# Two transformer-like blocks on one core: the end of the first block's experts, rebuilt, and the order of the second block's first slabs

## What is computed, cut to what matters here

```python
# peer_ffn, per token block of 128: for 8 heads the 16 best of 16384 experts
ue = jnp.take(u, eid, axis=0)
act = jax.nn.gelu(jnp.einsum('thkd,td->thk', ue, xt), approximate=False)
ve = jnp.take(v, eid, axis=0)
ff = jnp.einsum('thk,thkd->td', gate * act, ve)
h = layernorm(ALPHA * h + ff, ln2_g, ln2_b)      # end of block 1, ALPHA = 2 ** 0.25
x = h                                            # block 2
h = rmsnorm(x, norm1_gain_2); proj = h @ w_in_2
q_a, f_a, i_a, g_a, q_b, k_b, v_b, f_b = jnp.split(proj, ...)
```

## Time and profile before

| | |
|---|---|
| median of three runs | 3098.26 us |
| the profiled execution's own time | 3097.76 us |
| its span in the trace, mean granted clock | 3096.0 us, 0.985 |
| PE, PEld busy | 2666.7 us (86%), 1914.2 us (62%) |
| DVE, ACT, POOL busy | 1770.5 us (57%), 881.6 us (28%), 532.5 us (17%) |
| the chain that ended last | PE 60%, DMA 30%, DVE 5%, issue 3% |
| bytes moved | 859.94 MB, of them 536.90 by POOL's gathers |

### The profile page before, as it was taken

The page is one execution under the profiler, slowest core; times in us unless marked ns, Lnnn a source line. Parts: engine busy times, 40 slices in busy tenths (PEclk is TensorE's granted clock), DMA queues, the critical chain, the costliest instruction groups (busy, mean ns, idle before and its releaser), DMA issues.

```text
span 3096.0 us, 33400 instructions
## 1 busy us (share of the span) xinstructions
PE 2666.7 (86%) x12561; PEld 1914.2 (62%) x12561; DVE 1770.5 (57%) x2212; ACT 881.6 (28%) x943; POOL 532.5 (17%) x532
## 2 busy tenths in 40 slices
PE   6999998677777777777777777999999999999998
PEld 6999888622222222222222237998877888888886
DVE  5456556855555555555555456544656656555445
ACT  3433433300011111111111004433444444444443
POOL 0000000344433343333334430000000000000000
PEclk9999999899999999999999998999999999999999
DMA  6554563899999999999999995544454555555553
GB/s 228 169 172 160 180 228 136 341 422 421 421 422 422 422 422 422 422 422 422 422 422 422 422 356 179 175 156 151 143 190 155 189 190 189 189 189 190 190 193 146
DMA packets 220040, 859.94 MB, mean 278 GB/s; under 512 B 17616, under 2 KB 20016, under 8 KB 147120
## 3 DMA queue, kind: packets, MB, share of 16 engines
q0 software_dynamic: 73728, 536.90, 41.9%
q1 hardware_dynamic: 146224, 321.79, 31.1%
HBM read 856.54 MB, written 2.10 MB: 277 GB/s over the span
## 4 chain that ended last, share of the span: by engine, by line
PE 60%; DMA 30%; DVE 5%; issue 3%; ACT 1%; POOL 0%; POOLq 0%; DVEq 0%; ACTq 0%
DMA vb<-in_peer_v,vidx 29%; PE PS L462 11%; PE PS L2002 7%; PE PS L1860 7%; PE PS L464 5%; PE PS L491 5%; PE PS L495 5%; PE PS L493 5%; PE PS L503 4%; PE PS L507 4%; PE PS L505 4%; DVE wl L396 1%; ACT wh L391 1%; DMA ub<-in_peer_v,vidx 1%; PE PS L1876 1%
## 5 line engine op out<-in xcount | busy, mean ns | idle before, releaser
L1860 PE MATMUL PS<-vb,diag 128*128 128x512 f32 x1920 | 890.0, 607 | 331.4 <-DMA vb<-in_peer_v,vidx 317.3
L396 DVE TENSOR_TENSOR wl<-raw,wh 128x2048 fp32r<-128x2048 f32 x292 | 669.3, 2292 | 732.0 <-ACT wh L391 730.4
L1860 PEld LDWEIGHTS PS<-vb,diag 128*128 128x128 f32 x1920 | 346.3, 190 | 874.4 <-issue 750.6
L1358 DVE CUSTOM_DVE_ANT_0 ub<-ub,RES 128x2048 f32<-128x2048 f32 x256 | 586.5, 2292 | 479.0 <-DMA ub<-in_peer_u,uidx 475.1
L391 ACT CAST wh<-raw 128x2048 fp32r<-128x2048 f32 x292 | 556.7, 1907 | 912.8 <-PE PS L495 292.7
L462 PE MATMUL PS<-XHL,wh 128*128 128x512 f32 x1408 | 488.2, 394 | 0.0
L491 PE MATMUL PS<-XHL,wh 128*128 128x256 f32 x1408 | 402.2, 286 | 7.8 <-DVE XHL L537 4.8
L495 PE MATMUL PS<-XHL,wl 128*128 128x256 f32 x1408 | 399.6, 284 | 0.0
L493 PE MATMUL PS<-XHL,wh 128*128 128x256 f32 x1408 | 399.6, 284 | 0.0
L464 PE MATMUL PS<-XHL,wl 128*128 128x256 f32 x1408 | 390.0, 277 | 0.0
L689 POOL DMA_INDIRECT ub<-in_peer_u,uidx x256 | 261.9, 1023 | 648.2 <-DVE uidx L1346 528.7
(11 more groups left out here) (304 smaller groups left out, 2166.6 us busy)
## 6 DMA issues: line engine op xcount, KB each, us to landing
raw<-in_w_in SPq DMA_DIRECT2D x112, 1024.0 KB, 5.1
raw<-in_w_ffn_gate SPq DMA_DIRECT2D x44, 1024.0 KB, 5.2
raw<-in_w_ffn_up SPq DMA_DIRECT2D x44, 1024.0 KB, 5.1
raw<-in_w_ffn_down SPq DMA_DIRECT2D x44, 1024.0 KB, 4.8
raw<-in_w_out SPq DMA_DIRECT2D x32, 1024.0 KB, 5.1
raw<-in_peer_wq SPq DMA_DIRECT2D x16, 1024.0 KB, 5.1
ub<-in_peer_u,uidx POOLq DMA_INDIRECT x256, 16.5
vb<-in_peer_v,vidx POOLq DMA_INDIRECT x240, 15.3
```

Of the source, the lines that this page charges most:

```text
L396: dve.tensor_tensor(wl[u % 2][:], raw[u][:], wh[u % 2][:].bitcast(F32), ALU.subtract).then_inc(lo_full[u % 2], 1)
L1358: dve.tensor_tensor_reduce(ub[k % RING][:], ub[k % RING][:], RES[:, tb, :], 1.0, 0.0, ALU.mult, ALU.add, dots[:, tb, k:k + 1]).then_inc(S. ...
L1860: m = pe.matmul(PS[:, 4 * tb + b, :], diag[:, k, :], vb[k % RING][:, b * W:(b + 1) * W], start=start and k == 0, stop=False, skip_group_ch ...
```

## The change

- The four units of block 2's first slab are loaded before the experts; ACT and DVE split units 0 and 1 inside the expert stage (ACT after step 1, DVE after step 1 and after step 13). GAIN3 moves to another place (PH + 40, the scores of tb 1) and is loaded after the last selection (`uidx_ready` 16).
- Before the first v row PE writes ALPHA times RES into all eight banks, with a scaled identity (`adiag`). DVE's scaling of RES goes.
- DVE takes rows 13 and 14 of the last step, PE row 15. DVE's first row is a plain product.
- Token block 0: statistics and centring read PSUM. Token block 1: DVE adds bank by bank as PE's last row finishes each, statistics between. Both norms go in quarters of 512 columns, ACT squares each scaled quarter and sums it, NRM is made in quarters and turned quarter by quarter.
- PE multiplies units 0 and 1 for token block 0 before it turns token block 1, then for token block 1.
- Block 2's slabs come in the order v v f f q q; the steps of the recurrent mixer are one unit apart, from slab 6 unit 3 on instead of slab 5 unit 3.

`mm_tokens` is `mm_unit`'s token form for one token block, split off. DVE's and PE's plans of the second block shift as ACT's do. `wf_raw` and slab 1 now follow `last_full[1]` at once.

```diff
-DVE_ROWS = (5, 7, 9, 11, 14, 15)
+DVE_ROWS = (5, 7, 9, 11, 13, 14)
...
-GATES2, HEADS2, ATTN = 7, 11, 43
+GATES2, HEADS2, ATTN = 7, 27, 43
...
-    GAIN3 = at("GAIN3", 56, [D])
+    GAIN3 = at("GAIN3", PH + 40, [D])
+    adiag = at("adiag", PH + 48, [P])
...
+        w_in2 = w_view(inp["w_in_2"])
+        for u in range(UNITS):
+            load_unit(sp, S_IN2, u, w_in2[:, u * UC:(u + 1) * UC, 4 * W:5 * W])
         sp.wait_ge(S.scores_cp, 8)
         sp.dma_start(GAIN[:], row(inp["ln2_g"][0], D)).then_inc(S.norm_in, 16)
         sp.dma_start(BIAS[:], row(inp["ln2_b"][0], D)).then_inc(S.norm_in, 16)
-        sp.wait_ge(w_free[1], 2 * S_IN2)
+        sp.wait_ge(S.uidx_ready, 2 * H)
         sp.dma_start(GAIN3[:], row(inp["norm1_gain_2"][0], D)).then_inc(S.norm_in, 16)
         sp.wait_ge(last_full[1], 16 * (TOPK // RING))
-        w_in2 = w_view(inp["w_in_2"])
-        for u in range(UNITS):
-            load_unit(sp, S_IN2, u, w_in2[:, u * UC:(u + 1) * UC, 2 * W:3 * W])
-        sp.wait_ge(S.ffsum, 8)
         sp.dma_start(wf_raw[:], w_in2[:, :, 14 * W:14 * W + H]).then_inc(S.wf_in, 16)
         with sp.Fori(0, 1) as i:
             for u in range(UNITS):
-                load_unit(sp, i + S_IN2 + 1, u, w_in2[:, u * UC:(u + 1) * UC, ds(i * W + 3 * W, W)])
-        stream(S_IN2 + 2, w_in2, 0, 2)
-        stream(S_IN2 + 4, w_in2, 4 * W, 2)
+                load_unit(sp, i + S_IN2 + 1, u, w_in2[:, u * UC:(u + 1) * UC, ds(i * W + 5 * W, W)])
+        stream(S_IN2 + 2, w_in2, 2 * W, 2)
+        stream(S_IN2 + 4, w_in2, 0, 2)
...
+        act.activation(adiag[:], ident[:], ACT.Copy, scale=ALPHA).then_inc(S.base_diag, 1)
...
         weigh(1, 1)
+        lead(act, split_hi, S_IN2)
...
-        root(5, rstd[:, 0:1])
-        root(6, rstd[:, 0:1])
-        x_hi(act, 2, 0, 4)
-        split_hi(act, S_IN2, 0)
-        root(7, rstd[:, 1:2])
-        split_hi(act, S_IN2, 1)
-        root(8, rstd[:, 1:2])
-        x_hi(act, 2, 4, 8)
+        def z_squares(tb):
+            for q in range(4):
+                y = slice(q * W, q * W + W)
+                act.wait_ge(S.z_ready, 4 * tb + q + 1)
+                act.activation(NRM[:, 0, y], RES[:, tb, y], ACT.Square,
+                               accum_out=msq4[:, tb, q:q + 1]).then_inc(S.z_squared, 1)
+        for tb in range(TB):
+            root(5 + 2 * tb, rstd[:, tb:tb + 1])
+            z_squares(tb)
+            root(6 + 2 * tb, rstd[:, tb:tb + 1])
+            x_hi(act, 2, 4 * tb, 4 * tb + 4)
...
-        outs2 = [f_out] * 2 + [gq_out] * 2 + [tm_copy(G_V)] * 2 + [fqk_out(FQ, SCALE)] * 2 \
+        outs2 = [tm_copy(G_V)] * 2 + [f_out] * 2 + [gq_out] * 2 + [fqk_out(FQ, SCALE)] * 2 \
             + [fqk_out(FK, 1.0)] * 2 + [tm_copy(FV)] * 2 + [g_out]
         run_slabs(act, split_hi, S_IN2, 14, plan(
             [(j, 3, lambda j=j: outs2[j](S_IN2 + j)) for j in range(13)],
             [(0, 1, wf_split), (*slot(GATES2), lambda: gate_log(1, LA2[0:H, :]))],
-            [(1 + j, 0, lambda j=j: f_log(j)) for j in range(2)],
-            [(2 + j, 1, lambda j=j: b_exp(j)) for j in range(2)],
-            [(3 + j, 0, lambda j=j: nb_exp(j)) for j in range(2)],
-            [(*slot(HEADS2 + n), lambda n=n: g_step(n)) for n in range(H + 2)],
+            [(3 + j, 0, lambda j=j: f_log(j)) for j in range(2)],
+            [(4 + j, 1, lambda j=j: b_exp(j)) for j in range(2)],
+            [(5 + j, 0, lambda j=j: nb_exp(j)) for j in range(2)],
+            [(*divmod(HEADS2 + n, UNITS), lambda n=n: g_step(n)) for n in range(H + 2)],
...
+        split_lo(dve, S_IN2, 0)
         with dve.Fori(1, H - 1) as i:
             link.enter(i, 1, 50)
             for tb in range(TB):
                 expert_step(i * 2 + tb, tb, i + tb)
         link.leave(1, H - 2)
+        split_lo(dve, S_IN2, 1)
...
+            if k == DVE_ROWS[0]:
+                a = dve.tensor_scalar(RES[:, 1, :], ub[k % RING][:], ew[:, 1, k:k + 1], None, ALU.mult)
+            else:
+                a = dve.scalar_tensor_tensor(RES[:, 1, :], ub[k % RING][:], ew[:, 1, k:k + 1], RES[:, 1, :],
+                                             ALU.mult, ALU.add)
+            link(a, S.v_added)
+        def sum_stats(tb, q):
+            src = PS[:, q, :] if tb == 0 else RES[:, 1, q * W:(q + 1) * W]
+            return dve.bn_stats(stats[:, tb, q, :], src)
         def second_norms(tb):
-            for b in range(4):
-                a = row_stats(tb, b)
-            link(a)
             link(dve.bn_aggr(mv[:, tb, :], stats[:, tb, :, :]))
-            r1 = rstd[:, tb:tb + 1]
+            r1, m1 = rstd[:, tb:tb + 1], msq[:, tb:tb + 1]
             inverse_root(5 + 2 * tb, r1, mv[:, tb, 1:2], LN_EPS)
             dve.wait_ge(S.norm_in, 96)
-            link(dve.scalar_tensor_tensor(RES[:, tb, :], RES[:, tb, :], mv[:, tb, 0:1], GAIN[:],
-                                          ALU.subtract, ALU.mult))
-            link(dve.scalar_tensor_tensor(RES[:, tb, :], RES[:, tb, :], r1, BIAS[:], ALU.mult, ALU.add))
-            for b in range(4):
-                a = row_stats(tb, b)
-            link(a)
-            link(dve.bn_aggr(mv[:, tb, :], stats[:, tb, :, :]))
-            m1 = msq[:, tb:tb + 1]
-            link(dve.tensor_tensor(m1, mv[:, tb, 0:1], mv[:, tb, 0:1], ALU.mult))
-            link(dve.tensor_tensor(m1, m1, mv[:, tb, 1:2], ALU.add))
-            inverse_root(6 + 2 * tb, r1, m1, RMS_EPS)
-            dve.scalar_tensor_tensor(NRM[:, tb, :], RES[:, tb, :], r1, GAIN3[:], ALU.mult,
-                                     ALU.mult).then_inc(S.tm_ready, 1)
-        link(dve.tensor_scalar(RES[:, 1, :], RES[:, 1, :], ALPHA, None, ALU.mult))
+            parts = [slice(q * W, q * W + W) for q in range(4)]
+            for q, y in enumerate(parts):
+                src = PS[:, q, :] if tb == 0 else RES[:, 1, y]
+                dve.scalar_tensor_tensor(RES[:, tb, y], src, mv[:, tb, 0:1], GAIN[:, y], ALU.subtract,
+                                         ALU.mult).then_inc(S.z_centred, 1)
+            for q, y in enumerate(parts):
+                dve.wait_ge(S.z_centred, 4 * tb + q + 1)
+                dve.scalar_tensor_tensor(RES[:, tb, y], RES[:, tb, y], r1, BIAS[:, y], ALU.mult,
+                                         ALU.add).then_inc(S.z_ready, 1)
+            dve.wait_ge(S.z_squared, 4 * tb + 4)
+            link(dve.tensor_reduce(m1, msq4[:, tb, :], AX, ALU.add))
+            dve.tensor_scalar(r1, m1, 1.0 / D, RMS_EPS, ALU.mult, ALU.add).then_inc(S.square_ready, 1)
+            dve.wait_ge(S.root_ready, 7 + 2 * tb)
+            link(dve.reciprocal(r1, r1))
+            for y in parts:
+                dve.scalar_tensor_tensor(NRM[:, 0, y], RES[:, tb, y], r1, GAIN3[:, y], ALU.mult,
+                                         ALU.mult).then_inc(S.nrm_part, 1)
         dve.wait_ge(S.v_done, LAST * TOPK)
-        add_sums(0, ALPHA)
+        for q in range(4):
+            a = sum_stats(0, q)
+        link(a)
         second_norms(0)
         for k in DVE_ROWS[:2]:
             last_row(k)
         x_lo(dve, 2, 0, 4)
-        for k in DVE_ROWS[2:-1]:
+        for k in DVE_ROWS[2:]:
             last_row(k)
-        dve.wait_ge(S.acc_done, 1)
-        add_sums(1, 1.0)
-        last_row(DVE_ROWS[-1])
+        for q in range(4):
+            r = RES[:, 1, q * W:(q + 1) * W]
+            dve.wait_ge(S.acc_done, q + 1)
+            dve.tensor_tensor(r, r, PS[:, 4 + q, :], ALU.add).then_inc(S.ffsum, 1)
+            if q >= 1:
+                dve.wait_ge(S.ffsum, q)
+                sum_stats(1, q - 1)
+        dve.wait_ge(S.ffsum, 4)
+        link(sum_stats(1, 3))
         second_norms(1)
...
-        split_lo(dve, S_IN2, 0)
-        x_lo(dve, 2, 4, 5)
-        dve.wait_ge(S.tm_ready, 6)
-        split_lo(dve, S_IN2, 1)
-        x_lo(dve, 2, 5, 8)
+        x_lo(dve, 2, 4, 8)
         dve.wait_ge(S.xt_lo, 24)
...
+        pe.wait_ge(S.base_diag, 1)
+        for tb in range(TB):
+            for b in range(4):
+                pe.matmul(PS[:, 4 * tb + b, :], adiag[:], RES[:, tb, b * W:(b + 1) * W], start=True, stop=False,
+                          skip_group_check=True)
...
+        def turn_quarters(tb):
+            for q in range(4):
+                pe.wait_ge(S.nrm_part, 4 * tb + q + 1)
+                for c in range(4):
+                    m = pe.transpose(bank4(4 * tb + q)[:, c, :], NRM[:, 0, (4 * q + c) * P:(4 * q + c + 1) * P],
+                                     ident[:])
+                m.then_inc(S.xt_ps, 1)
         for j, k in enumerate(PE_ROWS):
             if j == 6:
-                turn_x(pe, 2, NRM, (0,))
+                turn_quarters(0)
             pe.wait_ge(last_full[k % RING], (k // RING + 1) * 16)
             pe.wait_ge(S.diag_ready, LAST * TOPK + j + 1)
             for b in range(4):
                 m = pe.matmul(PS[:, 4 + b, :], diag[:, k, :], ub[k % RING][:, b * W:(b + 1) * W],
                               start=False, stop=False, skip_group_check=True)
-            m.then_inc(S.v_done, 1)
```

(74 more changed lines are left out.)

29 lines of the change are left out of this document (11 added, 18 removed).

## The result

| | before | after |
|---|---|---|
| median of the runs | 3098.12 us (4 runs, 3096.56 to 3105.85) | 3124.15 us (4 runs, 3118.83 to 3130.20) |
| ratio to before, 95% interval | | 1.0079 (1.0059 to 1.0099) |
| profiled execution, its span | 3097.76, 3096.0 us | 3118.83, 3116.8 us |
| last v row of step 14 ends | 1809.94 | 1836.54 |
| statistics of token block 1 end (S) | 1863.33 | 1891.51 |

The change makes the kernel slower by 0.8%, where I had forecast 3090.5. All of it, and more, is lost in the expert stage, where I had forecast +2.5. The page after shows two things there.

What follows compares the result with a forecast made beforehand. Expert stage bound by its gathers, block 2 by TensorE; the change works on the 21.5 us gap between. +2.5 - 3.3 - 6.7 = -7.5 against 3097.76 gives 3090.3, stated as 3090.5; own range 3088 to 3093.5, wider 3084.5 to 3098.

Steps and rivals of the forecast that it cites:

- On VectorE one split ... 0, at worst 2: Expert stage: one split delays step 2's first dot some 7 us, but gathers in flight keep engines fed; 0, at worst 2.
- The slower one, head steps one unit apart: Block 2, rival: head steps stall because VectorE and ACT parts must fit one unit; 22 us, 3112; chance 0.10.
- GAIN3, +2.5: Expert stage: its 1 MB load, issued near 1703 us where DMA engines are full, delays gathers behind it by 2.5 us.
- Early units, base matmuls, ScalarE's copies, 0: Before the experts: early weight loads, residual matmuls into PSUM and ACT copies fall into idle time; cost 0.
- The end of the statistics, -3.3: Behind the experts: earlier gathers and TensorE taking row 15 end token block 1's statistics at 1860.0, 3.3 us earlier.
- Gather 9: POOL, last step, a sign: row 5 done early lets this gather start 1.1 us sooner and take near 1 us.
- my value of 5.3: TensorE's row 15 after an idle stretch near 5 us: 5.30 us, as row 10 took; bounds 3.6 and 5.3.
- From S to the first slab, -6.7: Norm of token block 1 to block 2's first slab's end: 31.6 us against 38.3, a gain of 6.7.
- Last product: Norm of token block 1 in quarters: its last product starts at S + 7.8.
- stall before unit 2: Block 2's first slab: weight buffer 0 comes free only at S + 14.8, so TensorE stalls 1.9 us.
- What was left of units 0 and 1: TensorE, after the transposes: the rest of both units' matmuls takes 5.4 us, to S + 17.5.
- the late last row: Rival: slab 1's loads and wf_raw's packets delay row 15, S 6 us later, 3096.5; chance 0.18 shared with idle preload.

Runs made afterwards that it cites:

- e1: The kernel before with one empty instruction more on VectorE right ahead of its expert loop; 3121.59 us, ratio 1.0065 to before.
- e2: The changed kernel with VectorE's split of unit 0 moved from ahead of the expert loop to right behind it; 3097.14 us, ratio 0.9983 to before.
- +12: The kernel before with 12 empty instructions on VectorE ahead of its expert loop; 3133.32 us, ratio 1.0096.
- e9: The kernel before with 123 empty instructions on VectorE ahead of its expert loop; ratio 1.0001.
- e4: The kernel of e2 with SyncE waiting for row 15, not row 13, before it issues wf_raw and slab 1's loads; ratio 0.9992.
- e7: The kernel of e4 with row 13 given to TensorE and row 15 to VectorE behind the adds; ratio 0.9978.
- e10: The kernel of e2 with TensorE's 24 first-token-block matmuls of units 0 and 1 put ahead of row 15; ratio 0.9981.
- e11: The kernel of e10 with GAIN3's load issued near the end of step 14 instead of behind the last selection; 3098.64 us, ratio 0.9977.
- e8: The kernel before with 122 empty instructions on VectorE ahead of its expert loop; ratio 1.0007.
- e13: The kernel before with 13 empty instructions on VectorE ahead of its expert loop; 3102.56 us, ratio 1.0011.

## Why the prediction was wrong

**The step that failed** is "On VectorE one split ... 0, at worst 2". I costed the split as work and looked for who waits for it; as work it costs at most the 1.7 us by which the changed kernel's +26.6 exceed e1's +24.9, and GAIN3's load is in these too. I didn't cost its place in the stream, a term that I put at nothing without a reason. It is 24.9 us, 5 at each of the five turns, in which 25 packets of 8 KB are fetched (e1: 1834.8 against 1809.9). It is shown from both sides, by e1 (put in without the change) and e2 (taken out of the change). No rival of mine had it. The slower one, head steps one unit apart, didn't happen: TensorE's idle time in the projections grew by 1.3 us only.

**What is bad about the place.** The runs show: 0 good, +1 bad, +12 bad, +13, +122 and +123 good. The built loop has 251 instructions, and each pass of the trace has 18 MATCH_VALUE_LOADs besides, 269 in all. If a fetch of 8 KB brings 128, the loop lies in three blocks, or in four when it starts in the last 12 places of one; three stay, four don't. That fits all six places and the stop of e1 ahead of the 13th instruction. I made it after e9 to fit what was known by then; only +12 and +13 were forecast by it, and both came true. The Trainium skill, "Runtime: NRT & Kernel Launch", section "Instruction fetch mechanics", gives most engines an instruction memory of 32 KiB, 512 instructions, and says that a taken branch whose target isn't held "forces a DMA fetch of the target page before execution can continue". By this the trace agrees: four blocks of 128 make 512, three for the loop and one for the fetch ahead, and five packets a turn are the loop's four blocks and one ahead. It names blocks of 16 KiB (256 instructions); on queue 14 the packets have 8 KB, and there the measurement decides. But that is the size of a packet. What is kept or dropped could still be two blocks of 256 instructions, the page's own size: a loop of 269 lies in two of them, or in three when it starts in the last 12 places of one, and all six places and the five packets fit that as well. The two accounts part at +129 to +140, bad by blocks of 128 and good by blocks of 256, which no run here has. That a fetch ahead takes a block's room is my reading, not shown. Nor is it shown why a stop lasts 7 us: that the packets have to wait beside full DMA queues, where gathers of u rows took 16.4 us from issue to landing in the page's median, is argued only.

**GAIN3, +2.5:** right. Step 14 ended 1.5 to 3.5 us later in e2, e4 to e7 and e10, and at 1810.36 without it (e11). By itself that would be weak, since it also ended 2.4 and 2.7 us later in e8 and e9, where GAIN3's load stays put; the 2.5 us of TensorE's waits in e2 (above) show it directly.

**Early units, base matmuls, ScalarE's copies, 0:** right within the scatter (568 to 604 us, windows above; first v row at 616.75, before at 615.43, in the other traces at 614.65 to 618.59).

**The end of the statistics, -3.3:** wrong, +1.6 (+1.2 in e2). The mis-sized term is the landing of a gather: I took 6.1 us from issue to landing for all rows, from row 14 of before, the quickest. In e2 rows 10 to 15 took 8.6, 8.8, 8.9, 8.7, 7.1 and 8.5 us by their waits. The trace before had said so for row 10, issued at 1833.62 and landed at 1841.07, 7.5 us:

```profile
1833.62 0.94 POOL L689 DMA_INDIRECT ub<-in_peer_v,vidx  x1 [0.30 <-issue]
```
 Gather 9 was near 1 us (0.94), as forecast, but row 10 came only 1.1 us earlier and not 2.6, and row 15 46 us behind step 14 and not 42.4. Then row 15 took 6.5 us in e2, between my value of 5.3 and the 7.1 that I had named for half clock; e10 shows 3.7 when the pause is filled. I had taken row 10 as the measure of what a pause costs; it isn't a steady one: after the same 2.93 us of idleness it took 5.30 us before, at a granted clock of 0.70, and 3.70 in e13, at 1.00.

**From S to the first slab, -6.7:** mechanism right, size 5.4. Last product S + 7.94 (7.8), first matmul S + 12.1 (12.0), stall before unit 2 1.66 (1.9). What was left of units 0 and 1 took 6.8 us, not 5.4: their first matmuls took 0.77 and 0.63 us instead of 0.39.

**Rivals:** the late last row happened (+4.9 against the forecast's S), though at most 0.7 of it by the loads that it named (e4). With all terms as measured but the fetches, the sum is +1.5 + 1.2 - 5.4 = -2.7; e2's ratio gives -5.3, and its interval, -9.6 to -1.2, holds the sum.

## What to carry to other kernels

A loop about as long as this one (251 built instructions, 269 on the chip; no other length was run), in a stage whose DMA queues are full, should be watched by the packet count of the instruction queues and by waits marked "issue" at its turn: an instruction added ahead of it can cost more than anything in the diff. Moving that one behind the loop gives it back (e2), and so should twelve empty ones more, by e13. So before judging a change that puts work ahead of such a loop, test the kernel before with as many empty instructions there as the change adds. And take a transfer's time from the slowest like row, not from the quickest.
